# Operand groups made in the phase ahead, states fetched in parts and later, loops written out: a hybrid decoder layer on one core

## What is computed

```python
proj = rmsnorm(h, attn_norm) @ w_in              # q k v z a b sB sC sh gA gB
o, S = gated_delta_rule(q, k, v, g, beta, s0)    # 32 heads, states 128 x 128
o = rmsnorm(o, gdn_norm) * silu(z)
y_a = o @ w_gdn_out                              # 4096 -> 2048
y_b = (sB * conv) @ w_sconv_out                  # 2048 -> 2048
mixed = sigmoid(gA) * y_a + sigmoid(gB) * y_b
h = h + mixed @ w_o
hn = rmsnorm(h, ffn_norm)
h = h + (silu(hn @ w_ffn_gate) * (hn @ w_ffn_up)) @ w_ffn_down
hn = rmsnorm(h, ple_norm)
h = h + sigmoid(hn @ w_ple_gate) * (p @ w_ple_proj)
y = rmsnorm(h, final_norm)
```

## Time and profile before

| | us |
|---|---|
| median of three runs (2705.9 to 2710.48) | 2707.32 |
| the profiled execution | 2707.02 |
| its span | 2705.5 |
| PE busy | 2622.2 |
| VectorE busy | 1656.9 |
| ScalarE busy | 1344.7 |
| mean granted clock of PE, share of full speed | 0.987 |

### The profile page before, as it was taken

How to read it: one execution, slowest core, us unless ns; L and a number is a source line. 1 busy time by engine, 2 the same in 40 slices (tenths; PEclk the granted TensorE clock), 3 DMA queues, 4 the chain that set the end, 5 groups by cost and what they waited for, 6 DMA issues and landing times.

```text
span 2705.5 us, 54636 instructions
## 1 busy us (share of the span) xinstructions
PE 2622.2 (97%) x21133; PEld 2582.7 (95%) x21133; DVE 1656.9 (61%) x2851; ACT 1344.7 (50%) x2024; POOL 463.2 (17%) x845
## 2 busy tenths in 40 slices
PE   6999999999999999999999998999999999999997
PEld 4999999999999999999999998999999999999897
DVE  4757677675767765533355564556775656776654
ACT  5546455464645544443444343355664546555653
POOL 1336162543616150000000000000110000110000
PEclk9999999999999999999999999999999999999998
DMA  5545465555546456677645556647996568985542
GB/s 167 168 142 164 140 181 142 167 148 165 162 139 189 137 164 191 180 209 205 197 163 168 182 168 226 193 141 226 318 313 206 188 189 256 315 271 181 178 154 80
DMA packets 441663, 505.25 MB, mean 187 GB/s; under 512 B 19521, under 2 KB 421690, under 8 KB 438658
## 3 DMA queue, kind: packets, MB, share of 16 engines
q1 hardware_dynamic: 415264, 415.42, 50.1%
q0 software_dynamic: 25664, 87.47, 10.4%
q10 hardware_dynamic: 578, 0.19, 0.0%
HBM read 477.10 MB, written 26.49 MB: 186 GB/s over the span
## 4 chain that ended last, share of the span: by engine, by line
PE 91%; DMA 3%; DVE 2%; POOL 1%; ACT 1%; issue 1%; ACTq 0%; DVEq 0%; SPq 0%; POOLq 0%
PE bank L684 90%; DMA raw<-in_w_o 1%; DMA raw<-in_w_ffn_down 1%; POOL sol L552 1%; POOL prod L549 1%; DVE wlo L1257 0%; DMA raw<-in_w_in 0%; ACT whi L962 0%; DMA vrow<-in_gdn_norm 0%; ACT xhi L976 0%; DVE h L1666 0%; PE bank L749 0%; PE bank L743 0%; PE bank L737 0%; DVE xlo L1278 0%
## 5 line engine op out<-in xcount | busy, mean ns | idle before, releaser
L684 PE MATMUL bank<-xhi,whi 128*128 128x264 f32 x5520 | 1600.0, 290 | 37.7 <-DVE wlo L1257 16.2
L684 PE MATMUL bank<-xlo,whi 128*128 128x264 f32 x5520 | 1573.9, 285 | 0.0
L684 PE MATMUL bank<-xhi,wlo 128*128 128x264 f32 x5520 | 1571.4, 285 | 0.0
L1257 DVE TENSOR_TENSOR wlo<-raw,whi 128x1024 fp32r<-128x1024 f32 x828 | 1010.9, 1230 | 776.8 <-ACT whi L962 775.8
L962 ACT ACTIVATE whi<-raw 128x1024 fp32r<-128x1024 f32 x828 | 872.4, 1058 | 861.3 <-PE bank L684 771.6
L684 PEld LDWEIGHTS bank<-xhi,whi 128*128 128x128 f32 x5520 | 1046.9, 190 | 41.7 <-issue 32.7
L684 PEld LDWEIGHTS bank<-xlo,whi 128*128 128x128 f32 x5520 | 1047.6, 190 | 0.7
L684 PEld LDWEIGHTS bank<-xhi,wlo 128*128 128x128 f32 x5520 | 1044.5, 189 | 0.0
L684 PE MATMUL bank<-ahi,whi 128*128 128x264 f32 x704 | 201.3, 286 | 3.8 <-DVE wlo L1257 3.8
L684 PE MATMUL bank<-ahi,wlo 128*128 128x264 f32 x704 | 201.2, 286 | 0.0
L684 PE MATMUL bank<-alo,whi 128*128 128x264 f32 x704 | 200.9, 285 | 0.0
(11 more groups left out here) (280 smaller groups left out, 1887.1 us busy)
## 6 DMA issues: line engine op xcount, KB each, us to landing
raw<-in_w_in SPq DMA_DIRECT2D x356, 512.0 KB, 3.9
raw<-in_w_ffn_gate SPq DMA_DIRECT2D x88, 512.0 KB, 5.0
raw<-in_w_ffn_up SPq DMA_DIRECT2D x88, 512.0 KB, 4.7
raw<-in_w_ffn_down SPq DMA_DIRECT2D x96, 384.0 KB, 2.9
raw<-in_w_gdn_out SPq DMA_DIRECT2D x64, 512.0 KB, 3.3
chunkS<-in_state_gdn POOLq DMA_DIRECT2D x16, 1024.0 KB, 7.3
raw<-in_w_sconv_out SPq DMA_DIRECT2D x32, 512.0 KB, 3.4
raw<-in_w_o SPq DMA_DIRECT2D x32, 512.0 KB, 3.3
```

The lines of the kernel that those rows point to most:

```text
L684: return pe.matmul(out, lhsT, rhs, start=start, stop=stop)
L1257: dve.tensor_tensor(wlo[:, at_ % SPLIT, :, :], raw[:, at_ % RAW, :, :], f32(whi[:, at_ % SPLIT, :, :]), ALU.subtract).then_inc(lo_ready, 1)
```

## The change

**The operand in groups.** For six phases xhi and xlo are now made in four groups of four tiles. Groups 0, 1 and 2 are made by hi_group and lo_group behind the weight splits of the last three pieces of the phase ahead (function makes; for pgate_first that phase is down1, with pproj in between), group i when the old tiles of group i have been used for the last time. Group 3 stays in the part "before" the phase. Where the source is still being written (wo, ffn0r, pgate_first), a group waits for its own two pairs alone.

**p.** Its transposes, phi and plo move from the opening of pproj into down1, behind its pieces 24 and 25.

**h and states.** h is fetched in four parts, each as soon as its two pairs of ya1 are through. The first two rounds of states are sent for at pieces 12 and 20 of wo. Those of the second half wait for both last stores, and for pieces 20 and 36 of down0.

**Loops.** All phases are written out on all engines, and waits are on constants.

```diff
+        MAKES = {"gates": "yb0", "yb1": "ya0", "ya0": "ya1", "ya1": "wo", "wo": "ffn0r", "down1": "pgate_first"}
+        XKEY = {"yb0": "yb", "ya0": "o0", "ya1": "o1", "wo": "mix", "ffn0r": "ffn", "pgate_first": "ple"}
+        GAIN = {"ffn0r": 320, "pgate_first": 336}
+        XSRC = {"yb0": lambda kt: yb[:, kt, :], "ya0": lambda kt: o_all[:, kt, :], "ya1": lambda kt: o_all[:, DTL + kt, :],
+                "wo": lambda kt: sgB[:, kt, :], "ffn0r": lambda kt: h[:, kt, :], "pgate_first": lambda kt: h[:, kt, :]}
+
+        def makes(ph, it, j):
+
+            i = j - (ph.pieces - 3)
+            return (MAKES[ph.name], i) if ph.name in MAKES and it == ph.iters - 1 and i >= 0 else (None, 0)
...
-            with pool.Fori(1, NB) as b:
+            for b in range(1, NB):
...
-            pool.wait_ge(xlo_ready, XR["mix"] + DTL)
-            pool.dma_start(h[:, :, :].rearrange("p k t -> p (k t)"), hT_d).then_inc(h_in, 16)
+            for q in range(4):
+                n = by["ya1"].q0 + 2 * q + 1
+                for m in (n - 1, n):
+                    pool.wait_ge(pair_free[m % 2], m // 2 + 1)
+                pool.dma_start(h[:, 4 * q:4 * q + 4, :].rearrange("p k t -> p (k t)"), hT_d[:, 4 * q * N:(4 * q + 4) * N]).then_inc(h_in, 16)
...
             for s in range(2):
+                pool.wait_ge(piece_used, by["wo"].p0 + 12 + 8 * s)
                 load(0, 0, s)
             for c in range(2):
-                with pool.Fori(0, NB // 2 - 1) as b2:
+                for b2 in range(NB // 2 - 1):
                     for s in range(2):
                         store(c, b2, s)
                         load(c, b2 + 1, s)
                 for s in range(2):
                     store(c, NB // 2 - 1, s)
-                    if c == 0:
+                if c == 0:
+                    for s in range(2):
+                        pool.wait_ge(piece_used, by["down0"].p0 + 20 + 16 * s)
                         load(1, 0, s)
...
+                if ph.name == "down1" and it * ph.pieces + j == 24:
+                    pe.wait_ge(p_in, 16 * (BLK + 1))
+                    for k in range(PD // P):
+                        for b in range(BLK):
+                            pe.transpose(bank[5 + k][:, b * P:(b + 1) * P], prow[:, b, k * P:(k + 1) * P], ident[:, :])
+                        m = pe.transpose(bank[5 + k][:, T:N], prow[0:NB, BLK, k * P:(k + 1) * P], ident[0:NB, 0:NB])
+                    m.then_inc(p_turned, 1)
...
-                elif ph.name == "pproj":
-                    pe.wait_ge(p_in, 16 * (BLK + 1))
...
+            def hi_group(name, i):
+
+                made_by = {v: k for k, v in MAKES.items()}[name]
+                if name == "yb0" and i == 0:
+                    freed_all(act, by["sb"])
+                elif name == "ya0" and i == 0:
+                    act.wait_ge(so_done, 1)
+                elif name in ("wo", "ffn0r", "pgate_first"):
+                    n = by[made_by].q0 + 2 * i + 1
+                    for m in (n - 1, n):
+                        act.wait_ge(pair_free[m % 2], m // 2 + 1)
+                if made_by == "down1":
+                    act.wait_ge(piece_used, by["down1"].p0)
+                else:
+                    act.wait_ge(piece_used, by[name].p0 - 3 + i)
+                for kt in range(KT * i, KT * i + KT):
+                    scale = {"scale": vec[:, GAIN[name] + kt:GAIN[name] + kt + 1]} if name in GAIN else {}
+                    act.activation(xhi[:, kt, :], XSRC[name](kt), ACT.Copy, **scale).then_inc(xhi_ready, 1)
 
...
+                name, i = makes(ph, it, j)
+                if name:
+                    hi_group(name, i)
+                if ph.name == "down1" and it * ph.pieces + j == 25:
+                    act.wait_ge(p_turned, 1)
+                    for k in range(PD // P):
+                        act.activation(phi[:, k, :], bank[5 + k][:, 0:N], ACT.Copy).then_inc(xhi_ready, 1)
...
-                elif name == "yb0":
-                    freed_all(act, by["sb"])
-                    plain_split(lambda kt: yb[:, kt, :], ph.p0)
-                elif name == "ya0":
-                    act.wait_ge(so_done, 1)
-                    plain_split(lambda kt: o_all[:, kt, :], ph.p0)
-                elif name == "ya1":
-                    plain_split(lambda kt: o_all[:, DTL + kt, :], ph.p0)
-                elif name == "wo":
-                    act.wait_ge(piece_used, ph.p0)
-                    freed_all(act, by["ya1"])
-                    plain_split(lambda kt: sgB[:, kt, :])
-                elif name == "ffn0r":
-                    act.wait_ge(piece_used, ph.p0)
-                    freed_all(act, by["wo"])
-                    scaled_hi(320)
+                elif name in XKEY:
+                    hi_group(name, 3)
                 elif name == "ffn1r":
                     act.wait_ge(piece_used, ph.p0)
-                elif name == "pproj":
-                    act.wait_ge(p_turned, 1)
-                    for k in range(PD // P):
-                        act.activation(phi[:, k, :], bank[5 + k][:, 0:N], ACT.Copy).then_inc(xhi_ready, 1)
-                elif name == "pgate_first":
-                    freed_all(act, by["down1"])
-                    scaled_hi(336)
...
+            def lo_group(name, i):
+
+                for kt in range(KT * i, KT * i + KT):
+                    dve.wait_ge(xhi_ready, XR[XKEY[name]] + kt + 1)
+                    if name in GAIN:
+                        m = dve.scalar_tensor_tensor(out=xlo[:, kt, :], in0=h[:, kt, :], scalar=vec[:, GAIN[name] + kt:GAIN[name] + kt + 1],
+                                                     in1=f32(xhi[:, kt, :]), op0=ALU.mult, op1=ALU.subtract)
+                    else:
+                        m = dve.tensor_tensor(xlo[:, kt, :], XSRC[name](kt), f32(xhi[:, kt, :]), ALU.subtract)
+                    m.then_inc(xlo_ready, 1)
...
-                        dve.wait_ge(h_in, 16)
+                        dve.wait_ge(h_in, 16 * 4)
...
+                name, i = makes(ph, it, j)
+                if name:
+                    lo_group(name, i)
+                if ph.name == "down1" and it * ph.pieces + j == 25:
+                    plain_split(XR["ple_p"], lambda k: bank[5 + k][:, 0:N], PD // P, (phi, plo))
...
-                elif name in ("yb0", "ya0", "ya1", "wo"):
-                    src = {"yb0": lambda kt: yb[:, kt, :], "ya0": lambda kt: o_all[:, kt, :],
-                           "ya1": lambda kt: o_all[:, DTL + kt, :], "wo": lambda kt: sgB[:, kt, :]}[name]
-                    if name == "yb0":
-                        freed_all(dve, by["gates"])
-                    plain_split(XR[{"yb0": "yb", "ya0": "o0", "ya1": "o1", "wo": "mix"}[name]], src)
...
-                elif name == "pgate_first":
-                    norm_split(XR["ple"], 336)
-
-            walk(dve, work, (mine,), dve_per)
+                elif name in XKEY:
+                    lo_group(name, 3)
+
+            walk(dve, work)
```

More of the change, by code:

```diff
@@ L55, in __init__ @@
     def __init__(self, sem):
-        self.sem, self.base, self.k, self.it, self.per = sem, 0, 0, None, 0
-    def enter(self, it, per):
-        self.base, self.k, self.it, self.per = self.base + self.k, 0, it, per
-    def leave(self, iters):
-        assert self.k == self.per, f"{self.k} increments in the body, not {self.per}"
-        self.base, self.k, self.it = self.base + self.per * iters, 0, None
+        self.sem, self.k = sem, 0
     def inc(self, ins):
@@ L70, in settle @@
     def settle(self, eng):
-        v = self.base + self.k
-        eng.wait_ge(self.sem, v if self.it is None else self.it * self.per + v)
+        eng.wait_ge(self.sem, self.k)
 class Pair:
@@ L363, in mul, with walk @@
             return it * n + c
-        def walk(eng, work, counts=(), per=None):
+        def walk(eng, work):
             for ph in phases:
                 work("before", ph, 0)
-                if ph.iters == 1:
-                    work("body", ph, 0)
-                else:
-                    with eng.Fori(0, ph.iters) as it:
-                        for c in counts:
-                            c.enter(it, per[ph.name])
-                        work("body", ph, it)
-                    for c in counts:
-                        c.leave(ph.iters)
+                for it in range(ph.iters):
+                    work("body", ph, it)
         def cur_of(ph, it):
@@ L454, in _ @@
             for ph in phases:
-                if ph.iters == 1:
-                    body(ph, 0)
-                else:
-                    with sp.Fori(0, ph.iters) as it:
-                        body(ph, it)
+                for it in range(ph.iters):
+                    body(ph, it)
             yo = O["y_prompt"]
@@ L965, in split_ahead @@
                 at_ = ph.p0 + j + AHEAD
-                if ph.iters == 1 and at_ >= PIECES:
+                if ph is phases[-1] and at_ >= PIECES:
                     return
@@ L972, in squares @@
```

(28 more changed lines are left out.)

5 lines of the change are left out of this document (removed).

## The result

The changed kernel takes 2671.12 us (median of 4 runs, 2670.5 to 2672.16) beside 2706.61 us for the kernel before in the same comparison: 0.987 of it, with a 95% interval of 0.9853 to 0.9887, or 35.5 us less. Forecast were 2667.0 (2661 to 2682).

The account below looks back on a forecast made before the run. TensorE bounds the kernel, so only its idle time and slow-clock stretches, 50.1 us, could be won. Less 1.5, 1.0 and 7.3 left over, that is 40.3 us: 2707.3 to 2667.0 us, range 2661 to 2682.

Parts of the forecast that it names:

- The openings, 18.6 us: At the openings of yb0, ya0, ya1 and wo, early groups would remove all PE gaps and slow clock, 18.6 us.
- Inside wo, 9.2 us: Inside wo, h in four parts and state rounds at pieces 12 and 20 would remove all 9.2 us.
- ffn0r, 1.5 us left: At ffn0r, PE would still wait 1.5 us of 6.1 for the first square, late on ScalarE.
- Evacuation through at +1.3: Step at ffn0r: the last pair's evacuation ends 1.3 us after wo's last piece, putting the first square at +4.4.
- down0, 1.0 us left: In down0, each of two state rounds would delay PE by 0.5 us, leaving 1.0 us of 6.7.
- The upper bound, 1.6 for each round: In down0, the count for piece 27 gave 0 to 1.6 us of PE wait per round; 0.5 was taken.
- pproj and pgate_first, 7.3 us left: Waits for the h addition, last evacuations and first square leave 6.5 us, plus 0.8 slow clock: 7.3 of 9.5.
- Too full: Rival: VectorE overfills the last three pieces, leaving gaps of 1.5 us at each of six openings; 2676 us, chance 0.13.
- Each round stalls like the old one: Rival: each round in down0 stalls PE as before, 2 x 6.7 us instead of 1.0; 2679 us, chance 0.17.
- Other leftovers: Rival: clock still falls at openings without PE waits, 14.1 us; 2681 and more, chance 0.04 shared with unusable early groups.
- The jumps do cost: Rival: removing loop jumps wins 3 us more and down0 has no stall; 2662 us, chance 0.04 for below 2662.
- the slow fetches: Rival: straight code's instruction fetches are held up by state transfers, costing 88 us; 2755 us, chance 0.03 for slower.

Follow-up runs that it names:

- the old fetch: Changed kernel with h fetched in one transfer behind wo's last xlo and all rounds of states sent as in the kernel before: 2683.92 us, 0.9911.
- the kernel with the squares first: Changed kernel with squares of h's first four tiles ahead of the last xhi group in ffn0r and pgate_first, other squares one piece earlier: 2664.45 us, 0.9848.

## Where the prediction was right, and where it was off

**The openings, 18.6 us.** Right: no gap is left, and taking the groups back costs 18.6 us in the lined-up traces (15.9 by the medians). VectorE's sample chain ended 0.4 us ahead of PE, as its 0.3 us said.

**Inside wo, 9.2 us.** Right, by the old fetch (9.1 us came back). Rounds went out at 1676.27 and 1699.52, and ScalarE waited 0.12 us longer than usual for one piece (0.9 and 0.6 us when the same kernel ran again, far inside the look-ahead too).

**ffn0r, 1.5 us left.** The mechanism was right, the term mis-sized: some 4 us are left (4.0 by the kernel with the squares first). Two steps failed. "Evacuation through at +1.3": I let it follow a group that ends at +0.9 and counted its 0.76 us for less. PE begins ffn0r at 1733.94, VectorE's group 2 ends at 1735.21 (+1.3) and the addition at 1735.89 (+1.95), so that each step behind it is 0.7 later and the first ones-matmul starts at +5.1 instead of +4.4. And I set no slow clock behind this gap, where it ran at 0.57 (1.7 us lost). Of ten profiles with this same gap of 2.03 or 2.04 us, seven have the slow clock behind it and three none, so either value would have been a guess.

**down0, 1.0 us left.** Mis-sized: 1.70 + 1.41 = 3.1 us. In the count for piece 27 its landing was put at 8.3 to 9.4 us behind the issue (2042.15), and ScalarE could only start on it at 2054.78, 12.6 us behind it; PE reached it at 13.4, not 11.6. The queue rows that I took the 0.27 MB in 6 us from the earlier trace rows lie inside a round; the changed kernel shows the same (q0 and q1, first from 2044 to 2050, then from 2050 to 2055):

```profile
q0 software_dynamic: 329, 1.53, 82.8%
q1 hardware_dynamic: 210, 0.20, 10.0%
...
q1 hardware_dynamic: 1221, 1.20, 74.4%
q0 software_dynamic: 87, 0.57, 27.9%
```

Behind it the weights are moved fast again, 1.20 MB in 5 us, and still ScalarE's piece was there only at the end of that stretch; why so late is not shown. The upper bound, 1.6 for each round, came out about right (1.70 and 1.41), but by luck: the landing was some 3 us later than counted and PE 1.8 us later, and the times printed with it (split by 11.8, PE at 11.6) give 0.2 and not 1.6. In the seven profiles with the rounds at 20 and 36 this term is 1.4 to 3.2 us.

**pproj and pgate_first, 7.3 us left.** Right in sum, partly by luck, since errors in its parts cancel. The wait for the h addition is 3.70 us (3.7 forecast), and the experiment that moves the groups away from it removes it. The wait for the square is 1.54 (2.2 forecast), the short one of 0.6 us is absent, the slow clock took 1.5 us (0.8 forecast): 3.9 + 1.5 + 1.7 = 7.1.

**Loops, 0.** Right: 0.9997. The instruction queue's 57% more bytes were not felt anywhere. The 28 jumps in stretches without a gap cost PE under 0.01 us each, so the difference of 0.1209 and 0.1205 us between matmuls isn't theirs. By the Trainium skill (Runtime: NRT & Kernel Launch, Instruction fetch mechanics) a taken jump out of the blocks at hand costs a fetch. Whether any of these jumps leaves the blocks at hand is not shown, and with thirty of them gone the median fell by 0.03%.

**The rivals.** "Too full" (2676) falls: the last three pieces left nothing at the four openings. "Each round stalls like the old one" falls by size, 1.6 for 6.7. "Other leftovers" falls at the openings, where the clock is 1.00, and the early groups are usable early, since these gaps are gone. "The jumps do cost" and the slow fetches fall by the kernel without loops (the former's sum, 3 us more won and 1.0 less left, is 2663 and not 2662). The miss of 5 us is 2.5 at ffn0r, 2.1 at down0, and 0.7 of the final ones-matmuls, less 0.2 at pproj.

## What to carry to other kernels

Make the operand of the next phase behind the current one's last pieces, but only as much as is wanted first: one group in four gave most of it here. Express the look-ahead in microseconds of the engine that splits (8.0 with pieces of 2.9 us, 4.4 with shorter ones, less if it has just waited), and send a large transfer where its measured hold on the weights is below that. Where a count gives a range, take its upper bound as the value. When work is moved ahead, look at what then stands first in the queue behind it: the squares, which wait for nothing, stood behind a group that did, and turning the two round was worth 4.0 us at one opening.

## What the runs showed of the hardware

- While a round of 2.1 MB moves on the software queue, the weights are nearly shut out: 0.20 MB beside 1.53 MB in 6 us. The wait outlasts that: from issue until ScalarE went on 12.6 us for 2.1 MB and 16.3 us for 4.2 MB in down0, and some 11.5 and 18.4 us in wo.
- The clock behind a gap doesn't follow from the gap's length. In the kernel before, 2.56 us at ya0 had a slow stretch behind it and 3.46 us at ya1 none; in the same kernel without loops, 2.28 us at ya0 had none and 3.10 us at ya1 one that lost 1.5 us. Behind the same gap of 2.03 us at ffn0r seven profiles of ten had one. Behind the same gap of 3.70 us at pproj, ten profiles lost between 1.3 and 2.7 us. A single such loss can't be forecast to better than 1 us from these runs.
- A taken jump of a hardware loop cost PE nothing measurable: 28 of them in 1235 us, two traces equal to 0.01 us in each of eight stretches.
